# Layer 0's projections with tiles of x that are loaded already turned, and with the modulation steps one tile later

## The reference

```python
sh_a, sc_a, ga, sh_f, sc_f, gf = split((silu(c) @ w_ada[l] + b_ada[l]), 6)   # the same with c_ctx for the context
h = x * (1 + sc_a) + sh_a
z = h @ w_in[l]                       # 1024 -> 1440
q_a, kv_a, k_rope, gq, gk, gv = split(z)
q  = rms_norm(q_a, g_q_a) @ w_q_b     # 384 -> 768
kv = rms_norm(kv_a, g_kv_a) @ w_kv_b  # 256 -> 1024
gq, gk = rms_norm(gq), rms_norm(gk)   # then 2-D rotary positions on q_rope, k_rope, gq, gk
```

## Time and profile before

| what | value |
|---|---|
| median of 3 runs | 3491.16 us (3483.05 to 3494.77) |
| the profiled execution | 3486.9 us, span 3485.0 us |
| mean granted TensorE clock | 0.958 |
| PE busy | 3167.9 us (91%) |
| DVE busy | 2616.4 us (75%) |
| ACT busy | 1777.9 us (51%) |
| POOL busy | 1340.8 us (38%) |
| layer 0's projections | about 5 to 385 us of the span |

### The profile page before, as it was taken

How to read it: one execution, slowest core, us unless ns; L and a number is a source line. 1 busy time by engine, 2 the same in 40 slices (tenths; PEclk the granted TensorE clock), 3 DMA queues, 4 the chain that set the end, 5 groups by cost and what they waited for, 6 DMA issues and landing times. The chain is left out here.

```text
span 3485.0 us, 44696 instructions
## 1 busy us (share of the span) xinstructions
PE 3167.9 (91%) x14900; PEld 2265.8 (65%) x14900; DVE 2616.4 (75%) x2451; ACT 1777.9 (51%) x2048; POOL 1340.8 (38%) x1043
## 2 busy tenths in 40 slices
PE   6999699998896999999969997999989699999995
PEld 3677455544484788888847774555438488888883
DVE  2344467677687899999968875777768799999996
ACT  2333233333411788888844443333341288888884
POOL 2111011111211777777742210111111287777772
PEclk9999799999997999999989997999999799999998
DMA  7775632221354989879953646312115589899865
GB/s 267 258 249 196 192 80 69 74 58 53 112 213 163 342 314 380 294 276 383 386 206 126 189 137 179 92 46 70 40 64 212 214 302 378 301 374 347 332 249 213
DMA packets 288169, 734.59 MB, mean 211 GB/s; under 512 B 62440, under 2 KB 169360, under 8 KB 236712
## 3 DMA queue, kind: packets, MB, share of 16 engines
q0 software_dynamic: 109328, 502.86, 38.8%
q1 hardware_dynamic: 164344, 182.16, 17.2%
q10 hardware_dynamic: 14368, 47.99, 3.8%
HBM read 723.65 MB, written 124.37 MB: 243 GB/s over the span
## 5 line engine op out<-in xcount | busy, mean ns | idle before, releaser
L2409 DVE TENSOR_TENSOR ex_wl<-ex_back,ex_wh 128x2048 fp32r<-128x2048 f32 x288 | 652.7, 2292 | 93.4 <-ACT ex_wh L2323 93.4
L1398 ACT ACTIVATE at_pt<-at_st 128x1024 f32<-128x1024 f32 x328 | 335.3, 1024 | 544.9 <-PE at_st L1312 544.2
L2323 ACT ACTIVATE ex_wh<-ex_back 128x2048 fp32r<-128x2048 f32 x288 | 551.2, 1919 | 30.6 <-PE ex_vp L2254 17.2
L1457 DVE TENSOR_REDUCE at_nm<-at_sc 128x1 f32<-128x1280 f32 x246 | 365.5, 1486 | 206.6 <-PE at_sc L1274 203.8
L1471 DVE TENSOR_TENSOR at_acc<-at_acc,at_pt 128x1024 f32<-128x1024 f32 x256 | 317.1, 1239 | 102.0 <-ACT at_pt L1398 99.9
L2409 DVE TENSOR_TENSOR ex_wl<-ex_front,ex_wh 128x2048 fp32r<-128x2048 f32 x144 | 324.7, 2294 | 11.5 <-ACT ex_wh L2323 11.5
L2323 ACT ACTIVATE ex_wh<-ex_front 128x2048 fp32r<-128x2048 f32 x144 | 275.2, 1922 | 84.5 <-SPq L2192 60.3
L1339 PE MATMUL at_op<-at_pt,at_va 128*64 128x512 f32 x1280 | 307.8, 610 | 0.2
L2152 POOL DMA_INDIRECT ex_back<-in_w_down,piece_of x144 | 277.8, 1929 | 48.0 <-issue 43.4
L1312 PE MATMUL at_st<-at_q,at_km 96*128 96x512 f32 (+3 forms) x1008 | 265.8, 404 | 4.5 <-DVE at_nm L1457 4.0
L1312 PEld LDWEIGHTS at_st<-at_q,at_km 96*128 96x128 f32 (+1 forms) x1008 | 179.2, 192 | 97.5 <-issue 55.2
(11 more groups left out here) (316 smaller groups left out, 6682.0 us busy)
## 6 DMA issues: line engine op xcount, KB each, us to landing
ad_w<-in_w_ada POOLq DMA_DIRECT2D x48, 1024.0 KB, 12.0
heads<-T SPq DMA_DIRECT2D x80, 512.0 KB, 6.6
at_q<-heads SPq DMA_DIRECT2D x80, 256.0 KB, 4.2
at_km<-heads SPq DMA_DIRECT2D x16, 640.0 KB, 10.2
mr_ot<-o_s SPq DMA_DIRECT2D x18, 512.0 KB, 5.5
h_s<-mr_h ACTq DMA_DIRECT2D x18, 512.0 KB, 2.7
cy<-y_s POOLq DMA_DIRECT2D x9, 1024.0 KB
at_rinv<-inv_s POOLq DMA_DIRECT2D x68, 128.0 KB, 2.9
```

Of the source, the lines that this page charges most:

```text
L1398: nc.scalar.activation(pt[:, j % PT, :, 0:nq], st[:, j % 2, :, 0:nq], ACT.Exp).then_inc(exp_done, 1)
L1457: nc.vector.tensor_reduce(nm[:, v % 3, s:s + 1], bank[:, 0:kb * P], AX.X, ALU.max, negate=True).then_inc(max_done, 1)
L2323: nc.scalar.activation(wh[:, q], early.raw(u, p), ACT.Copy).then_inc(hi_done, 1)
L2409: nc.vector.tensor_tensor(wl[:, q], early.raw(u, p), wh[:, q].bitcast(F32), ALU.subtract).then_inc(lo_done, 1)
```

## The change

The host lays x and ctx out once more, as `x_turned`: 10 tiles of 128 features x 8 x 128 tokens. Layer 0 loads its tiles from there. `part_x` is no longer called in layer 0, and `modulate` reads `xt` in SBUF in place of `tp`. As `tp` is no longer freed ahead of `part_x`, `part_heads` waits for `lo_done` itself. The modulation steps: step 2 stands behind the split matmuls of tile 1 (where step 3 was), step t+1 in tile t, step 11 behind `part_qa` of the last tile. POOL waits for the up weights ahead of `ad_load(2)`, and its order is new. SyncE's wait for the stores of `ad_row` moves behind the stores of the last tile.

```diff
+        def turned_x(k):
+            return xt[:, k * P:(k + 1) * P] if first_layer else tp[k // 4][:, k % 4, :]
@@ sync
                     sp.dma_start(ada[:, :, j, :], ad_row[32 * j:32 * j + 2, :, :]).then_inc(ad_stored, 16)
-                sp.wait_ge(ad_stored, 65)
...
             put_v(t, R["tail_stored"])
+            if first_layer:
+                sp.wait_ge(ad_stored, 65)
@@ gpsimd
             if first_layer:
+                pool.wait_ge(w_loaded, 33)
                 ad_load(2)
                 norm_low(0)
-                for t in range(1, NT):
+                norm(0)
+                ad_load(3)
+                norm_low(1)
+                for t in range(2, NT):
+                    ad_load(t + 2)
                     norm(t - 1)
-                    if t == 1:
-                        ad_load(3)
-                    if t + 3 < AD_STEPS:
-                        ad_load(t + 3)
                     norm_low(t)
                 norm(NT - 1)
@@ scalar
             def load_x(t):
...
+                act.dma_start(xt[:, :], A["x_turned"][bass.ds(t, 1)].rearrange("a p k n -> p (a k n)")).then_inc(x_loaded, 16)
...
             def modulate(t):
-                act.wait_ge(x_full, 2 * t + 2)
+                if first_layer:
+                    act.wait_ge(x_loaded, 16 * (t + 1) + 1)
+                else:
+                    act.wait_ge(x_full, 2 * t + 2)
...
-                    nc.scalar.activation(dst, tp[0][:, k, :], ACT.Identity,
+                    nc.scalar.activation(dst, turned_x(k), ACT.Identity,
...
             if first_layer:
-                act.wait_ge(x_full, 3)
                 load_x(1)
...
-                        act.wait_ge(x_full, 2 * t + 3)
                         load_x(t + 1)
@@ vector
             def modulate(t):
...
-                    nc.vector.tensor_scalar(dst, tp[1][:, k - 4, :],
+                    nc.vector.tensor_scalar(dst, turned_x(k),
...
-                if first_layer and first:
-                    ad_take(2)
                 if step is not None:
                     ad_take(step)
...
-                behind(t - 1, first, None if first_layer or last else t + 1, t + 2 if first_layer else None, t if last else None)
+                behind(t - 1, first, None if first_layer or last else t + 1, t + 1 if first_layer else None, t if last else None)
...
-            behind(NT - 1, order=LAST)
+            behind(NT - 1, step=AD_STEPS - 1 if first_layer else None, order=LAST)
@@ tensor
-                    if tail or i >= 2:
+                    if first_layer or tail or i >= 2:
                         pe.wait_ge(lo_done, 4 * t + i)
...
-            part_x(0, lambda b: None)
+            if not first_layer:
+                part_x(0, lambda b: None)
...
             def tile(t, first=False, last=False):
                 if not first:
                     part_qa(t - 1)
-                if first:
+                if first_layer:
+                    if not first:
+                        part_ad(t + 1)
+                elif first:
                     part_x(t, lambda b: pe.wait_ge((mod0, mod1)[b], 5))
                 else:
                     part_x(t, lambda b: pe.wait_ge(lo_done, 4 * t - 4 + b))
-                if first_layer:
-                    part_ad(2 if first else t + 2)
...
                 if first_layer and first:
-                    part_ad(3)
+                    part_ad(2)
...
             part_qa(NT - 1)
+            if first_layer:
+                part_ad(AD_STEPS - 1)
             part_up(NT - 1)
@@ kernel
+    rows = np.concatenate([np.asarray(inputs["ctx"])[0], np.asarray(inputs["x"])[0]])
+    turned = np.ascontiguousarray(rows.reshape(NT, P, KC, P).transpose(0, 3, 2, 1))
+    arrays["in_x_turned"] = turned
+    A["x_turned"] = nc.dram_tensor("in_x_turned", turned.shape, F32, kind="ExternalInput").ap()
```

More of the change, by code:

```diff
@@ L645, in modulate @@
             def modulate(t):
-                dve.wait_ge(x_full, 2 * t + 3)
+                if first_layer:
+                    dve.wait_ge(x_loaded, 16 * (t + 1) + 1)
+                else:
+                    dve.wait_ge(x_full, 2 * t + 3)
                 dve.wait_ge(z_full, 3 * t + 1)
@@ L846, in part_x @@
             def part_x(t, free):
-                if first_layer:
-                    pe.wait_ge(x_loaded, 16 * (t + 1) + 1)
-                else:
-                    pe.wait_ge(x_ready, t + 2)
+                pe.wait_ge(x_ready, t + 2)
                 for b in range(2):
```

## The result

The kernel after takes 3460.64 us (median of 4 runs, 3455.16 to 3463.01); the kernel before took 3492.97 us beside it (4 runs, 3483.05 to 3500.82). The ratio is 0.9906, 95% interval 0.9882 to 0.9929: faster by 32.3 us, 0.9%. The forecast was 3457, range 3445 to 3472. The profiled execution of after is 3460.31 us (span 3458.4).

What follows compares the result with a forecast made beforehand. TensorE was taken to bound tiles 2 to 9, with waits in the first tile, tile 1 and the tail. Terms summed to 32.4 us: 3454.5 from the profiled execution, 3458.8 from the median; 3457 taken, range 3445 to 3472.

Steps and rivals of the forecast that it cites:

- a, the transposes: Layer 0, tiles 2 to 9: taking away 8 transposes of x a tile saves 0.97 us each tile, 7.8 us in all.
- b: First tile of layer 0: the transposes of x(0) are not late for anything; removing them is worth 0.
- c: First tile: gating step 2's load lets projection weights land sooner; z(0) starts 2.5 us earlier, two later waits save 1.3.
- d: From z(0) to z(1): x(1) and step 2 no longer lie between, about 0.9 us of wait remains; gain 3.7 us.
- its rival: First tiles: the weights are no faster, so c gives 0 and d 0.8; 6.7 us less gain, 3461 us; chance 0.09.
- e, the hole: Tile 1: step 2, weights present, replaces step 3, whose weights were late, 12.8 us; full clock afterwards, 1.7 us.
- f: Later modulation steps, each one tile later: same number, 3.6 us each, and the requests have slack; worth 0.
- g, the tail: End of layer 0's projections: SyncE's last heads go out without the wait for landing; 2.6 us, ends 2.6 and -1.9.
- The gain is carried to the end: Behind layer 0's projections: layer 1 keeps its code and everything starts from the stage's stores, so all 32.4 us stay.
- longer spans behind the stage as a sign of being wrong: After layer 0's projections: the prediction would be wrong if later spans were longer than before; no size given.
- The rival that ended slower: Tiles 2 to 9: modulation weights late for TensorE each tile; over 3497 us needs 43 us, 5.4 a tile; chance 0.01.

## Why the prediction was right

Its sum was 32.4 us; the medians give 32.3, and the stage 30.4 in the first pair of profiles. By its steps:

- *a, the transposes:* 7.8 expected. The lead is 108.45 - 86.58 = 21.87 us at the heads' transposes in tile 1 and 361.67 - 332.82 = 28.85 at the last part_qa, so 7.0 measured. The shape is right. The size is 0.84 us a tile and not 0.97, because the modulation step now starts 0.64 us behind part_qa's start (94.22 to 94.86), where the first transpose came 0.1 us sooner. ScalarE's slices from SBUF took 0.43 us each against 0.39 from PSUM; TensorE did not see it.
- *b:* right; the first tile is set by ScalarE's slice.
- *c and d, weights and the way to z(1):* 2.5 + 1.3 + 3.7 = 7.5 expected, 71.40 - 63.93 = 7.5 measured. The up weights landed at 54.6, 54 expected. The assumption that the weight queue alone would fill the engines holds: from 39 to 54 us, where no modulation weights are under way in the kernel after, the DMA share is 0.98 (392 GB/s), and 1.02 (417 GB/s) without the gate; so the trace agrees with the rule of the Trainium skill ("DMA: Bandwidth & Descriptors") that stood beside it. The price of its rival was too low: without the gate the stage lost 10 us, not 6.7, since the longer gap brought the slow clock, which the rival's sum left out.
- *e, the hole:* 12.8 + 1.7 = 14.5 expected, (108.45 - 86.58) - 7.5 = 14.4 measured. The number was right and the reading incomplete. I named one cause, the late request; there was a second wait under it, the bank that VectorE emptied only at 88.3. It did no harm to the forecast only because step 2 needs neither. The 1.7 for the slow clock is not in every execution either: in the third profile of the kernel before, the up projection behind the hole took 6.67 us and not 8.35 (98.84 to 105.51), at a clock of 1.00.
- *f:* worth nothing, right: a period is full on TensorE, and POOL sits idle for 6.23 us ahead of its requests in tile 9 (below), waiting for TensorE to free the buffers.
- *g, the tail:* 2.6 expected, 1.5 measured. The failed part is that the requests keep their 1.06 us each; right behind the stores of the modulation rows they took 1.35 (5.39 / 4).
- *The total:* the median of before moved by up to 5.3 us between the sets of runs (3489.37 to 3494.66), so the agreement to 0.1 us is partly luck. The stage says more of the sum, and it is below it: 2.0 in the first pair of profiles, 3.3 by the means of three.
- *"The gain is carried to the end", and longer spans behind the stage as a sign of being wrong:* in the first pair they are longer, 30.4 us of lead become 26.6. POOL's slow pattern in layer 1 accounts for 6 us of that pair, and no step of the prediction had it.

The rival that ended slower did not come. Its mechanism can be looked for in tile 9, where POOL's requests and VectorE's modulation lie over one another. POOL's timeline of the kernel after, one request a row, then VectorE's, then the first request of that tile in the kernel before:

```profile
302.63 0.76 POOL L414 DMA_DIRECT2D ad_w<-in_w_ada  x1 [6.23 <-PE adp L937]
303.50 0.71 POOL L414 DMA_DIRECT2D ad_w<-in_w_ada  x1
```

```profile
302.45 0.60 DVE L656 TENSOR_SCALAR hP<-xt,modt 128x128 f32<-128x128 f32 x2
302.96 0.60 DVE L656 TENSOR_SCALAR hS<-xt,modt 128x128 f32<-128x128 f32 x2
```

```profile
306.32 0.76 POOL L410 DMA_DIRECT2D ad_w<-in_w_ada  x1
```

The request that lay beside the modulation took 0.76 us, the ones behind it 0.71. The first request of a tile took 0.76 in the kernel before too, where VectorE's head norm and not the modulation lay beside it. The Trainium skill, "SBUF — State Buffer", section "SBUF: two separate sides", says that a VectorE instruction in its two-port mode, such as a float32 copy within SBUF, locks POOL out of writing descriptors while it runs. If it did so here, it is not seen in more than 0.05 us of a request, where the rival needed 16 us a tile.

## What to carry to other kernels

A row that names the releaser of a wait names the last one only: here an early request alone gained 3 to 7 us, and 13 to 14 once the bank was emptied early too. Before a request is made earlier, ask for each other thing the waiting instruction needs (the bank, the buffer, the copy that empties it) when it is ready, and in which queue behind what. A gap of TensorE of 4 us cost 3 more by the clock, one of 0.7 us nothing: price a rival's wait with what follows it. And a transfer that nobody needs soon should wait for the ones that are needed now; one line did that here for 6 to 10 us. Last, look at one pair of profiles as one draw: the stage's gain was 30.4 us in the first pair and 29.1 by the means of three.

## What was not expected of the hardware

- POOL's requests in the expert stages run in one of two patterns (490 or 553 us busy in 650), by something that differs between executions of one program. Most stages keep one pattern throughout; one changed over some 500 us in.
- Two 128x128 float32 slices with scale and shift took VectorE 0.60 us from SBUF (rows above) and ScalarE 0.86, which needs 0.78 for the same from PSUM. I had expected one price for either engine.
- The same four head requests took 5.39 us where they followed the four stores of the modulation rows within 0.05 us (5.52 in another execution), 4.87 where they came 0.44 us behind them, and 4.23, 0.8 of it a wait for VectorE, where they came 1.1 us behind them, in the run with the early first tile, which has no wait for landing either. With the wait, 2.6 us behind, they took 4.24. So it goes with the distance to the stores ahead and not with the wait itself. With those stores on POOL's queue they took 5.06, 0.67 of it a wait for VectorE. What lengthens them was not tried.
